# A mixture-of-experts decoder trunk: the shared expert's down products move from the end of each expert loop into the loop's own passes

## The reference, cut to what matters

```
scores = sigmoid(x2 @ w_router);  idx = top_k(scores + bias, 6)
gate   = 2.5 * scores[idx] / sum(scores[idx])
routed = sum over the six chosen experts e of
         gate_e * ((silu(x2 @ w_gate[e]) * (x2 @ w_up[e])) @ w_down[e])
shared = (silu(x2 @ w_sh_gate) * (x2 @ w_sh_up)) @ w_sh_down
x      = layer_norm(alpha * x + routed + shared)
```

## Time and profile before

| | |
|---|---|
| three runs | 1962.19, 1962.34 and 1968.25 us, median 1962.34 us |
| the profiled execution | 1960.34 us, its span 1958.6 us |
| mean granted TensorE clock | 0.981 |
| busy: TensorE, VectorE, ScalarE, GpSimd | 91%, 38%, 20%, 18% of the span |
| expert loop of the first layer, first gate product to last down product | from 384 to 892 us |
| expert loop of the second layer | from 1404 to 1911 us |

### The profile page before, as it was taken

The page is one execution under the profiler, slowest core; times in us unless marked ns, Lnnn a source line. Parts: engine busy times, 40 slices in busy tenths (PEclk is TensorE's granted clock), DMA queues, the critical chain, the costliest instruction groups (busy, mean ns, idle before and its releaser), DMA issues. The chain is left out here.

```text
span 1958.6 us, 36214 instructions
## 1 busy us (share of the span) xinstructions
PE 1788.3 (91%) x12636; PEld 1106.6 (57%) x12637; DVE 749.4 (38%) x2168; ACT 384.5 (20%) x882; POOL 354.6 (18%) x450
## 2 busy tenths in 40 slices
PE   9999999899998989879999969999889999997877
PEld 7888445456665555543444438754456666664442
DVE  4222754633332323224255553516623333332225
ACT  2112651011111111102265243211011111110001
POOL 8442000011111111110012712200011111111110
PEclk9999999999999999999899989999999999999999
DMA  6220225599999999999122220206899999999997
GB/s 228 79 82 23 97 90 218 213 411 421 421 421 421 421 422 420 421 421 354 55 65 76 65 42 3 70 19 260 327 413 415 422 421 421 420 421 422 422 416 307
DMA packets 144184, 541.80 MB, mean 277 GB/s; under 512 B 31030, under 2 KB 68498, under 8 KB 94302
## 3 DMA queue, kind: packets, MB, share of 16 engines
q1 hardware_dynamic: 122782, 490.20, 62.5%
q0 software_dynamic: 21312, 50.37, 6.6%
HBM read 521.58 MB, written 46.14 MB: 290 GB/s over the span
## 5 line engine op out<-in xcount | busy, mean ns | idle before, releaser
L718 PE MATMUL bank<-W,XT 128*64 128x256 f32 x2880 | 326.6, 383 | 36.9 <-DMA W<-in_w_exp_up_dram 17.8
L718 PEld LDWEIGHTS bank<-W,XT 128*64 128x64 f32 x2880 | 233.9, 138 | 139.9 <-DMA W<-in_w_exp_gate_dram 28.9
L755 PE MATMUL bank<-W,ht 128*64 128x512 f32 x720 | 166.1, 602 | 13.1 <-DMA W<-in_w_exp_down_dram 8.3
L2256 PE MATMUL bank<-XT,room 128*128 128x512 f32 x352 | 158.6, 605 | 0.0
L729 DVE TENSOR_TENSOR sig<-sig,bank 128x256 f32<-128x256 f32 x72 | 30.3, 421 | 268.1 <-ACT sig L725 234.6
L718 PE MATMUL bank<-room,XT 128*64 128x256 f32 x864 | 103.2, 391 | 15.6 <-DMA room<-in_w_exp_gate_dram 7.8
L731 DVE TENSOR_TENSOR h<-sig,bank 128x256 f32<-128x256 f32 x72 | 30.4, 422 | 214.9 <-PE bank L718 214.9
L2256 PEld LDWEIGHTS bank<-XT,room 128*128 128x128 f32 x352 | 66.2, 193 | 82.1 <-issue 81.9
L784 POOL DMA_INDIRECT y_rows<-y,row x36 | 36.7, 1020 | 419.0 <-DVE y L777 419.0
L784 POOL DMA_INDIRECT y_rows<-XT,row x36 | 36.4, 1010 | 412.2 <-DVE XT L777 412.2
L704 ACT ACTIVATE XT<-bank 128x512 f32<-128x512 f32 x74 | 44.2, 597 | 329.8 <-PE bank L696 329.8
(11 more groups left out here) (490 smaller groups left out, 2780.1 us busy)
## 6 DMA issues: line engine op xcount, KB each, us to landing
W<-in_w_exp_gate_dram SPq DMA_DIRECT2D x88, 1024.0 KB
W<-in_w_exp_up_dram SPq DMA_DIRECT2D x88, 1024.0 KB
W<-in_w_exp_down_dram SPq DMA_DIRECT2D x88, 1024.0 KB
room<-in_w_exp_gate_dram SPq DMA_DIRECT2D x40, 1024.0 KB
third_high<-in_w_exp_down_dram SPq DMA_DIRECT2D x40, 1024.0 KB
W<-y_rows SPq DMA_DIRECT2D x24, 1024.0 KB, 13.4
third_up<-in_w_exp_up_dram SPq DMA_DIRECT2D x20, 1024.0 KB
w_shg<-in_w_exp_up_dram SPq DMA_DIRECT2D x20, 1024.0 KB
```

The source lines that it names most:

```text
L718: last = pe.matmul((gate, up)[m][64 * a:64 * a + 64, :], xt[s][:, k, 64 * a:64 * a + 64], weights(w, a, m)[:, k * FE:(k + 1) * FE], start= ...
L755: last = pe.matmul(B[5 + half][64 * a:64 * a + 64, :], ht[:, j, 64 * a:64 * a + 64], weights(w, a, 2)[:, at:at + 512], start=(j == 0), sto ...
L2256: last = pe.matmul(main(i)[:], wc[i % WBUFS][:, kb, :], K.XT[:, kb, :], start=(kb == 0), stop=(kb == KD - 1))
```

## The change

The shared down product is cut into 16 units, each 256 columns of one token tile. Since the number of turns is known only at run time (16 to 40), a table `K.due` holds 0 or 1 for each turn: the last 16 turns are due, the earlier ones multiply by zero and change nothing. In every turn ScalarE copies, after y of the first pass, the hidden values of the unit's tile, scaled by 0 or 1, and makes the factor (1 or alpha) (`stage_hidden`); TensorE makes the unit's two products between the gate and the up products of the second pass, into bank 5, once y of the pass before is copied out (`shared_product`); VectorE forms x * factor + product in `K.X` between its two products for h (`add_shared`); TensorE's down products of that pass wait for it. The shared down weights get a buffer of their own and are loaded on SP's queue as the first transfer of the loop, ahead of the third pair's down weights. At the end, the shared products and the scaling of X are gone; `row_product` starts the banks itself. y has one buffer, so the copies of pass n wait for the scatter of pass n - 1. The sigmoid is written into h's buffer, in place of one of its own. Some constants move into memory that is used later, are made in fewer columns or in bfloat16, and two small ones are added.

```diff
-        y = [xt_room[:, 0:D], sb("y1", [P, D])[:]]
+        y = xt_room[:, 0:D]
...
-        sig, h = sb("sig", [P, FE]), sb("h", [P, FE])
+        h = sb("h", [P, FE])
...
+        sh_down = sb("w_sh_down_kept", [P, 2 * D])
+        staged_hidden = sb("staged_hidden", [P, 2, P])
...
         def loop(eng, body):
 
+            before = eng.value_load(K.plan_turns[0:1, 1:2], min_val=0, max_val=MAX_PASSES // 2 - UNITS)
             for u in range(2):
-                body(u, u)
+                body(u, u, 0, before)
...
+        def unit_of(turn, before):
+            return (before + turn) & (UNITS - 1)
+
+        def stage_hidden(act, turn, before):
+            wait_from(act, shared_added, turn)
+            act.activation(due[:], K.due[:, bass.ds(before + turn, 1)], ACT.Copy).then_inc(due_kept, 1)
+            act.wait_ge(due_kept, turn + 1)
+            act.activation(factor[:], due[:], ACT.Copy, bias=1.0, scale=ALPHA - 1.0)
+            at = ((before + turn) & (UNITS - D // UNIT)) * (P * UNIT // D)
+            act.activation(staged_hidden[:], shared.hidden[:, :, bass.ds(at, P)], ACT.Copy, scale=due[:, 0:1]).then_inc(hidden_staged, 1)
+
+        def shared_product(pe, n, turn, before):
+            pe.wait_ge(shared.loaded, 16)
+            pe.wait_ge(hidden_staged, turn + 1)
+            pe.wait_ge(y_a, n)
+            at = (unit_of(turn, before) & (D // UNIT - 1)) * UNIT
+            for j in range(2):
+                last = pe.matmul(B[5][:, 0:UNIT], staged_hidden[:, j, :], shared.w[:, j, bass.ds(at, UNIT)], start=(j == 0), stop=(j == 1))
+            last.then_inc(shared_made, 1)
+
+        def add_shared(dve, turn, before):
+            dve.wait_ge(shared_made, turn + 1)
+            x = X_flat[:, bass.ds(unit_of(turn, before) * UNIT, UNIT)]
+            dve.scalar_tensor_tensor(x, x, factor[:], B[5][:, 0:UNIT], ALU.mult, ALU.add).then_inc(shared_added, 1)
...
                 last.then_inc(done, 1)
+                if m == 0 and s == 1:
+                    shared_product(pe, n, shared_turn, before)
...
+            if s == 1:
+                add_shared(dve, shared_turn, before)
             dve.wait_ge(gate_up_done, n + 1)
...
+        def down(pe, s, n, turn, w, shared_turn):
+            if s == 1:
+                pe.wait_ge(shared_added, shared_turn + 1)
...
         def keep_y(eng, s, n, half):
-            wait_from(eng, stored[s], through(n - 2, s))
+            wait_from(eng, stored[1 - s], through(n - 1, 1 - s))
...
+                shared.load_down(sp, sh_down[:])
                 third_pair = experts_of(WSLOTS - 1)
...
     def load_early(self, sp):
-        self.shared.load_down(sp, self.down_room)
         self.ln.load(sp)
...
-    def products(self, pe):
-        pe.wait_ge(self.shared.loaded, 16)
+    def products(self, pe, y_a, y_d, passes):
         for t in range(2):
-            self.shared_product(pe, t)
             self.row_product(pe, t, 0)
             self.row_product(pe, t, 1)
-        pe.wait_ge(self.scaled, 1)
         self.row_product(pe, 0, 2)
         self.row_product(pe, 1, 2)
-        self.shared_product(pe, 2)
-        self.row_product(pe, 2, 0)
-        self.row_product(pe, 2, 1)
-        self.row_product(pe, 2, 2)
-        self.shared_product(pe, 3)
+        for y_kept in (y_a, y_d):
+            pe.wait_ge(y_kept, 1)
+            pe.wait_ge(y_kept, passes)
+        for q in range(ROW_PAIRS):
+            self.row_product(pe, 2, q)
         self.turn(pe, 0)
...
-        for t in range(NT):
-            dve.tensor_scalar_mul(X[:, t, :], X[:, t, :], ALPHA).then_inc(self.scaled, 1)
```

More of the change, by code:

```diff
@@ L210, in make @@
             step(pool.tensor_tensor(K.level[:, lv, :], K.level[:, lv, :], K.upto[:], ALU.mult))
-        for q in range(4):
-            step(pool.tensor_copy(K.masks4[:, q * P:(q + 1) * P], (K.upto if q % 2 else K.before)[:]))
+        for q in range(3):
+            step(pool.tensor_copy(K.masks3[:, q * P:(q + 1) * P], (K.before if q % 2 else K.upto)[:]))
         for t in range(NT):
@@ L901, in _ @@
                 pe.wait_ge(xt_a, held(pe, turns * 2 + 1))
-                ending.products(pe)
+                ending.products(pe, y_a, y_d, held(pe, turns * 2))
             @block.scalar
@@ L906, in _, with one_pass @@
                 keep_xt(act, 0, 0, 0)
-                def one_pass(n, u):
+                def one_pass(n, u, turn, before):
                     sigmoid(act, n)
@@ L911, in one_pass @@
                     keep_y(act, u, n, 0)
+                    if u == 0:
+                        stage_hidden(act, turn, before)
                     if isinstance(n, int) and n == 0:
@@ L927, in _, with one_pass @@
                 start = step.n
-                def one_pass(n, u):
+                def one_pass(n, u, turn, before):
                     step = Chain(dve, steps, start + n * PASS_STEPS)
-                    hidden(dve, n, step)
+                    hidden(dve, u, n, step, turn, before)
                     keep_xt(dve, 1 - u, n + 1, 1)
@@ L996, in load @@
             sp.wait_ge(K.out_stored, 16 * NT)
-    def shared_product(self, pe, t):
-        B, shared = self.K.banks, self.shared
-        for half in range(2):
-            for j in range(2):
-                pe.matmul(B[2 * t + half][:], shared.hidden[:, j, t * P:(t + 1) * P], shared.w[:, j, half * 512:(half + 1) * 512],
-                          start=(j == 0), stop=False)
     def row_product(self, pe, t, q):
```

73 lines of the change are left out of this document (43 added, 30 removed).

## The result

The changed kernel takes 1976.06 us (median of 19 executions) where the kernel before, run beside it on the same chip, takes 1967.30 (19 executions): ratio **1.0040, 95% interval 1.0028 to 1.0052**. It is slower by some 8 us, and the forecast was 7 us faster. A second series gave 1.0023 (1.0006 to 1.0041). The profiled execution took 1978.43 us around a span of 1976.7. That of the kernel before was a low one of its own spread (1960.34, while 35 executions in one series ran from 1957.15 to 1975.90), so the two profiles differ by 18.1 us where the medians differ by 8.8.

What follows compares the result with a forecast made beforehand. Transfers were taken to bound the loops, and TensorE's shared products the ends. Layers of -4.7 and -2.2 us sum to -6.9, bringing the median of 1962.34 to 1955.4 us; range 1950 to 1961.

Steps and rivals of the forecast that it cites:

- The loop's passes: Second passes of both loops: TensorE's added products, mostly hidden by transfers, cost 0.8 us in the first, 3.0 in the second.
- The columns: Two added 256-column products in each second pass: 0.91 us of TensorE, bounds 0.91 and 1.8, plus a 0.31 us count read.
- Transfers bound the loop as a whole: Both loops: they end when their bytes are moved, at 420 to 422 GB/s; added TensorE time costs only if the queue empties.
- The end: After each layer's last scatter lands (T): rows become the bound, last sum at T + 23.1, gaining 5.5 and 5.2 us.
- Rival 3: End of each layer: TensorE's clock stays low, last sum at T + 30.8, +8.5 us in all, 1970.8; chance 0.07.
- The loop's beginning: Shared weights as SP's first transfer, 2.5 us, mostly fit unused room; 0.2 and 0.5 us remain, bounds 0 and 2.5 each.
- One buffer of y: Loop copies waiting for the previous pass's scatter: usually no wait, at most 0.3 us, and no cost.
- VectorE's and ScalarE's additions: In the loop: VectorE's sum (at most 0.69 us) and ScalarE's three copies (at most 3 x 0.60) are hidden.
- Rival 2: Beginnings of both loops: the queue runs dry more often, costing 3 and 6 us, total 1960.6; chance 0.18.
- Its own signs of being wrong: Loop windows below 410 GB/s beyond 100 us; clock 0.50 in over two end pairs; sums at T + 18 or after T + 26; middle passes above 13.7 us.

Runs made afterwards that it cites:

- e3: The kernel before with only the second buffer of routed results taken away, so copies wait for the previous pass's scatter: ratio 1.0019 to the kernel before.
- e9: The kernel before with only the changed kernel's constants (three masks for four, tables and a scratch in the expert weights' room): ratio 0.9996 to the kernel before.
- e1: The changed kernel without the loop's shared products, VectorE's addition and ScalarE's copies: ratio 1.0016 to the kernel before.
- e13: e1 with 12 small products in a branch never taken, which the compiler dropped: ratio 1.0011 to the kernel before.
- e14: e1 with 42 small products in a branch never taken, which the compiler dropped: ratio 1.0014 to the kernel before.
- e16: The changed kernel without the loop's products, with 12 never-run products behind a branch in each second-pass body (36 per layer): ratio 1.0027 to the kernel before.
- e2: The changed kernel with each unit's product and addition cut from 256 columns to 16, all instructions and waits kept: ratio 1.0032 to the kernel before.
- e17: e16 with 40 never-run products behind each branch in place of 12: ratio 1.1179 to the kernel before.
- the order alone: Pair 7 in place of pair 5 as the first with two passes, in either kernel: ratio to the kernel before 0.9975 for the changed, 0.9978 for the before.

## Why the prediction was wrong

**The failed step is "The loop's passes".** It priced the hole of the earlier trace rows as TensorE's lateness from three added products and a count read, 0.8 us in the first loop and 3.0 in the second, and put the loading of the added code at nothing, without a reason. Against the three kernels that have the loops of before (before, e3, e9: means 509.9 and 512.5) the two profiles of the changed one (520.9 and 516.8) lost 10.9 and 4.3. With the ends' 3.4 us a layer (below) that makes 15.2 - 6.8 = 8.4 us, and some 8 were measured. The first loop's loss is the step's failure: stops for code, as (1) shows. The second's 4.3 us cannot be pinned to the change: the three kernels with the loops of before range from 508.7 to 516.6 there, and e1, e13 and e14, without any product, take 517.3 to 517.8. Three things were missed.

(1) *Code.* The step asked what the added instructions take on TensorE, not what they take to be loaded. The row was there: 5.36 us of "issue". I used it for the clock that followed and never asked what stopped TensorE in the third pass. e16 shows that the length of the code in the branches, without any of the work, costs 6.4 of the 10.9 us of the first loop (its 36 products are a stand-in: their code need not be as long as that of the change, though both bring one packet). The Trainium skill, "Runtime: NRT & Kernel Launch", section "Instruction fetch mechanics", says that code is fetched in 16 KiB blocks, one after the other, and that a taken branch to code outside the two blocks held stops the engine until it is fetched. By that rule, the trace agrees at two of the six branches: packets of that size at their first entries, with stops of 1.9 to 5.2 us. It was the rule that spoke against the change, and the prediction leaves it out.

(2) *The hole stood closer to both loops than the profile showed.* The earlier trace rows gave 401 GB/s, a queue hardly empty, and I took that for the usual case. The two kernels with the same passes and 9.1 and 11.0 us of stops took 512.1 and 516.6 us for the second loop; its profile had 6.5 and 508.7. A sum made against a single execution inherits its luck: 3.0 us was the price from there, and the average stands elsewhere.

(3) *The columns* were priced at 0.91 us and a read; a turn lengthened by 1.3. Of the loss they are the smaller part: e2 took them away and got 2.1 and 0.9 us back, in the first loop hardly more than the 1.9 us by which the two profiles of the changed kernel differ. What the rest of the first loop's 10.9 us is, beside 6.4 for code and 2.1 for columns, no run separates.

Point by point, the rest:

- *Transfers bound the loop as a whole*: right. From 160 to 480 us into a loop no 20-us window of any kernel here but e17 stands under 404 GB/s, and the median is 421 or 422; a loop's length follows from how long the queue stood empty ahead of that. But where the forecast was that added TensorE time is hidden, the cover is thin in one place above all, and that place decides.
- *The end*: the mechanism was right, the size too large. Rows come at 402 and 411 GB/s, a pair each 2.55 us, and VectorE is not later. The last sum came at T + 24.0 in the second layer, forecast T + 23.1, a gain of 4.3 for 5.2. In the first it came at T + 26.0, a gain of 2.6 for 5.5: TensorE waited 2.19 us for the last pair's rows, and its products fell into a stretch at half clock (0.75 in the window from 936 to 938; 3.15 us for 1.94). Over the kernels with either form the ends average 37.3 and 33.9, 3.4 us per layer.
- *Rival 3, a low clock at the end*: only in that last pair. While TensorE worked 15.47 of 22 us and 14.76 of 21, idling 0.6 us ahead of each pair, the granted clock was 1.00.
- *The loop's beginning*: the shared weights filled what was unused; 370 and 389 GB/s in the first 14 us for 354 and 360. Right so far; whether the rest of the 2.5 us cost anything is not separated from the passes.
- *One buffer of y, VectorE's and ScalarE's additions*: no wait shows; e3 leaves at most 0.35% open, and its profile gives no wait to put them to.
- *Rival 2* had the right place and the wrong price: the queue ran dry at both loops' beginnings, for 15 us in sum and not 9.
- *Its own signs of being wrong*: two came, windows below 410 GB/s beyond the first 100 us of a loop (269 from 1516 to 1526, which is 97 to 107 us in) and passes of 14.14 us in the middle, where 13.7 was the limit. The first layer's last sum, at T + 26.0, stands at the limit of a third.

What stays open: why a load of code takes TensorE 2 to 5 us when its packet takes 0.9 to 1.1 us, and why only two of the six first entries show a stop. That the fetch stands in line behind the weights would fit, but no run tried it.

## What to carry to other kernels

A loop fed by a saturated queue has its slack where the issuing engine pauses, not on the average: find the longest pause, and count all that can make the consumer late ahead of it, first entries into branches among them. Code copied into several branches of a loop body can stop the engine where a copy is entered the first time (here at two of six), so keep in the branches only what differs, and place the irregular work behind the turns in which code still comes in. A remedy is also to be tried on the kernel before: here the order alone made both kernels equally fast. Before pricing a term of a few us, look at more than one execution: here the profile that the sum was built on was one of the kernel's luckiest (of 168 timed executions of it, 7 took no longer).

## What the hardware showed that I had not expected

TensorE's loop code stays where it is once loaded, up to a size: with 7 or 8 packets of 16 KB per loop no further packet comes in the remaining 400 us and more. With 120 products behind the branches in place of e16's 36 (e17), the execution has 165 packets in place of 62, nearly all the added ones in the second loop, which took 735.4 us in place of 513.7. The section of the Trainium skill named above gives TensorE 128 KiB for code, eight such blocks. By that rule the changed kernel's loop, with 8 packets, stands right at the edge, and the trace agrees in where the loading becomes endless; that the first loop of e17 still got by with nine packets at its beginning, no run explains. The Trainium skill speaks there also of a FIFO of only two lines and of no instruction cache; the loops here, which load nothing after their first 75 us, say otherwise.
